# Branch sums in six PSUM banks and another order of the second block's rope factors, splits and taps

## What is computed

```python
# first block
h = rms_norm(x, mix_norm_g)
proj = h @ w_in                          # 1024 x 8708: four attentions' q, k, v and a gate of 4 x 1024
ys = mixers(proj)                        # stick-breaking, dilated, forgetting, differential: 4 x 256 wide
branch = einsum('bsnc,ncd->bsnd', ys, w_branch)
x = x + sum_n(sigmoid(gate_n) * branch_n) @ w_out
x = x + square(relu(rms_norm(x, mlp_norm_g) @ w_up)) @ w_down
x = rms_norm(x, final_norm_g)
# second block
h = rms_norm(x, norm1_g)
q, k, v, u = split(h @ w_in_2)           # 512, 512, 512, 2 x 512
q, k = rope(rms_norm(q)), rope(rms_norm(k))      # per head of 64
attn = causal_softmax_attention(q, k, v)         # 8 heads, one block of 256 keys
a, g = split(u + glu_b);  h = a * sigmoid(g)
conv = silu(layer_norm(causal_depthwise_conv31(h) + dw_b))
x = x + concat(attn, conv) @ w_out_2
x = x + (silu(h2 @ w_gate_2) * (h2 @ w_up_2)) @ w_down_2   # h2 = rms_norm(x, norm2_g)
```

## Time and profile before

| | |
|---|---|
| median of 3 runs | 815.37 us |
| the profiled execution | 815.08 us, its span 813.3 us |
| TensorE busy | 785.4 us, 97% of the span |
| VectorE busy | 476.2 us, 59% |
| ScalarE busy | 407.0 us, 50% |
| GpSimd busy | 41.8 us, 5% |
| read from memory | 134.43 MB, 167 GB/s over the span |
| mean granted TensorE clock | 0.998 of 2.4 GHz |

### The profile page before, as it was taken

How to read it: one execution, slowest core, us unless ns; L and a number is a source line. 1 busy time by engine, 2 the same in 40 slices (tenths; PEclk the granted TensorE clock), 3 DMA queues, 4 the chain that set the end, 5 groups by cost and what they waited for, 6 DMA issues and landing times.

```text
span 813.3 us, 9724 instructions
## 1 busy us (share of the span) xinstructions
PE 785.4 (97%) x3930; PEld 659.4 (81%) x3930; DVE 476.2 (59%) x623; ACT 407.0 (50%) x542; POOL 41.8 (5%) x38
## 2 busy tenths in 40 slices
PE   7999999999999899999999998998999999999998
PEld 5887889888888687888888887776987888888896
DVE  6654364757765867554445447688956645445534
ACT  6565455455656536455444445555455543443341
POOL 1000000000000410000000004011000000000000
PEclk9999999999999999999999999999999999999999
DMA  9842424434445355655655554835113755655341
GB/s 336 310 156 92 141 78 156 155 116 144 156 157 205 114 184 192 222 185 174 207 182 180 187 176 148 318 127 190 54 52 104 259 173 190 204 160 205 103 156 53
DMA packets 68508, 136.25 MB, mean 168 GB/s; under 512 B 2416, under 2 KB 7152, under 8 KB 67824
## 3 DMA queue, kind: packets, MB, share of 16 engines
q1 hardware_dynamic: 68000, 134.44, 48.3%
q10 hardware_dynamic: 464, 1.20, 0.4%
HBM read 134.43 MB, written 1.05 MB: 167 GB/s over the span
## 4 chain that ended last, share of the span: by engine, by line
PE 82%; DVE 9%; ACT 4%; issue 2%; POOL 1%; DMA 0%; ACTq 0%; SPq 0%; DVEq 0%
PE b L574 19%; PE b L576 18%; PE b L575 18%; PE SS L574 4%; PE SS L576 4%; PE SS L575 4%; PE TT L543 4%; DVE ca L1956 2%; DVE wlo L1492 2%; PE OO L576 2%; PE OO L574 2%; PE OO L575 2%; ACT whi L1054 1%; PE SS L657 1%; PE b L714 1%
## 5 line engine op out<-in xcount | busy, mean ns | idle before, releaser
L1492 DVE TENSOR_TENSOR wlo<-raw,whi 128x2048 fp32r<-128x2048 f32 (+2 forms) x123 | 273.8, 2228 | 160.2 <-ACT whi L1054 160.0
L1054 ACT CAST whi<-raw 128x2048 fp32r<-128x2048 f32 (+2 forms) x123 | 227.3, 1850 | 125.8 <-PE b L576 86.9
L574 PE MATMUL b<-whi,Ahi 128*128 128x512 f32 (+2 forms) x568 | 222.8, 392 | 3.1 <-DVE wlo L1492 1.8
L576 PE MATMUL b<-whi,Alo 128*128 128x512 f32 (+2 forms) x568 | 216.2, 381 | 0.0
L575 PE MATMUL b<-wlo,Ahi 128*128 128x512 f32 (+2 forms) x568 | 215.7, 380 | 0.0
L574 PEld LDWEIGHTS b<-whi,Ahi 128*128 128x128 f32 x568 | 107.9, 190 | 23.4 <-issue 2.5
L576 PEld LDWEIGHTS b<-whi,Alo 128*128 128x128 f32 x568 | 107.5, 189 | 20.8
L575 PEld LDWEIGHTS b<-wlo,Ahi 128*128 128x128 f32 x568 | 108.0, 190 | 18.5
L574 PE MATMUL b<-whi,Bhi 128*128 128x512 f32 x168 | 66.9, 398 | 3.0 <-DVE gates L1758 2.7
L576 PE MATMUL b<-whi,Blo 128*128 128x512 f32 x168 | 65.5, 390 | 0.0
L575 PE MATMUL b<-wlo,Bhi 128*128 128x512 f32 x168 | 65.5, 390 | 0.0
(11 more groups left out here) (270 smaller groups left out, 1000.0 us busy)
## 6 DMA issues: line engine op xcount, KB each, us to landing
raw<-in_w_in SPq DMA_DIRECT2D x40, 1024.0 KB, 4.9
raw<-in_w_up SPq DMA_DIRECT2D x16, 1024.0 KB, 5.4
raw<-in_w_dn SPq DMA_DIRECT2D x16, 1024.0 KB, 4.9
raw<-in_w_d SPq DMA_DIRECT2D x11, 1024.0 KB, 5.0
raw<-in_w_g SPq DMA_DIRECT2D x10, 1024.0 KB, 5.0
raw<-in_w_u SPq DMA_DIRECT2D x10, 1024.0 KB, 4.9
raw<-in_w_out SPq DMA_DIRECT2D x8, 1024.0 KB, 4.9
raw<-in_w_br SPq DMA_DIRECT2D x4, 1024.0 KB, 5.0
```

What stands on the lines that cost most here:

```text
L574: e.matmul(dst, xh, H[:, kc, c0:ce], start=first and kc == krs[0], stop=False)
L576: ins = e.matmul(dst, xl, H[:, kc, c0:ce], start=False, stop=last and kc == krs[-1])
L1054: e.copy(whi[:, s, 0:m], raw[:, r, 0:m]).then_inc(s_hi, 1)
L1492: e.tensor_tensor(wlo[:, s, 0:m], raw[:, r, 0:m], whi[:, s, 0:m].bitcast(F32), ALU.subtract).then_inc(s_lo, 1)
```

## The change

- **Banks.** The 16 groups of the branch stage go over six banks, 7, 0, 1, 2, 3, 4, instead of three; the two explicit entries of `gone` for banks 1 and 2 are dropped, since those banks' last branch groups are now recorded by the loop.
- **Timetable of the second block.** The turn of the gate half and its sigmoid (`gt`, `gs`) stand two groups later, the turn of the value half (`ut`) one group later, the gating `ug` at the same groups as before; the first two turns of rotated q (`r2`) one group earlier. Taps before the attention are 7 + 2 + 4 + 2 instead of 4 + 2 + 1 + 1.
- **Order on VectorE.** A rope factor stands before the group's split, `ug` behind everything else. In the norm steps the split stands between the gain product and the low part. At chunk 0 a split stands between the two parts of the statistics.
- **Order on ScalarE.** At chunk 0 the cast of the unit stands before the last turn's steps and the four final squares. The table of exponentials is loaded behind group 7.
- **Attention.** Six taps a head instead of seven; the rounds 8 and 9 of TensorE are written out, with the seventh head's product before the eighth head's turn.

```diff
--- before.py
+++ after.py
@@ -64,9 +64,12 @@
          9: [(0, "v", 1280, None)]}
 
 QP = [(c, col, dst, sc) for c in range(10) for col, kind, dst, sc in PAIRS[c] if kind == "qk"]
+
 CH2 = [(2048, 512), (1536, 512), (0, 512), (512, 512), (1024, 512)]
 HC2 = [4, 4, 4, 4, 4, 2]
 W_ACC = {(0, 0): 3, (1, 0): 4, (0, 1): 7, (1, 1): 0}
+
+BR = [7, 0, 1, 2, 3, 4]
 FIRST = [(0, 0), (1, 0), (0, 1), (1, 1)]
 PLAIN = [(0, 0), (0, 1), (1, 0), (1, 1)]
 
@@ -129,19 +132,21 @@
 def timetable2():
 
 
-    bg = {s: [] for s in range(24)}
-    bg[3] += [("gt", 0)]
-    bg[4] += [("gs", 0), ("gt", 1)]
-    bg[5] += [("gs", 1)]
-    bg[7] += [("ut", 0)]
-    bg[8] += [("ut", 1), ("ug", 0)]
-    bg[9] += [("ug", 1)]
-    for i, (a, b, c) in enumerate(((11, 13, 15), (12, 14, 16), (15, 17, 18), (16, 18, 19))):
+    bg = {s: [] for s in range(20)}
+    bg[5] += [("gt", 0)]
+    bg[6] += [("gs", 0), ("gt", 1)]
+    bg[7] += [("gs", 1)]
+    bg[8] += [("ut", 0), ("ug", 0)]
+    bg[9] += [("ut", 1), ("ug", 1)]
+    for i, (a, b, c) in enumerate(((11, 13, 14), (12, 14, 15), (15, 17, 18), (16, 18, 19))):
         bg[a] += [("r0", i), ("ra", i)]
         bg[b].append(("r1", i))
         bg[c].append(("r2", i))
-    for s, n in ((10, 4), (11, 2), (13, 1), (14, 1)):
+    for s, n in ((10, 7), (12, 2), (14, 4), (18, 2)):
         bg[s].append(("cv", n))
+    rank = {"r1": 0, "ug": 0, "r0": 1, "ra": 1}
+    for s in bg:
+        bg[s].sort(key=lambda x: rank.get(x[0], 2))
     return bg
 
 
@@ -781,7 +786,7 @@
             for n in range(4):
                 for t in range(2):
                     g = 8 * hf + 2 * n + t
-                    bk = g % 3
+                    bk = BR[g % 6]
                     w.wait_ge(s_xl, X["B", t, n // 2] + 1)
                     clear(bk)
                     product(("br", hf, n, t), Bhi, Blo, 4 * (n // 2), t, lambda c0, bk=bk: bank[bk], True, True,
@@ -841,8 +846,6 @@
                     tail(k)
 
 
-        gone[1] = (s_gm, 14)
-        gone[2] = (s_gm, 15)
         for j in range(8):
             def turn_h(j=j):
                 for t in range(2):
@@ -948,16 +951,20 @@
             conv(n_conv[0])
             n_conv[0] += 1
 
-        for k in range(10):
-            if k < 8:
-                az(k)
-                tile_part()
-            if 1 <= k < 9:
+        for k in range(8):
+            az(k)
+            tile_part()
+            if k:
                 at(k - 1)
-            if k < 4 or k > 7:
+            if k < 4:
                 tile_part()
             if k > 1:
                 ap(k - 2)
+        tile_part()
+        ap(6)
+        at(7)
+        tile_part()
+        ap(7)
         tile_part()
         for t in range(2):
             key = ("Y", t, 0)
@@ -1397,16 +1404,19 @@
 
         for i in range(5):
             for q, (ui, t) in enumerate(PLAIN):
-                if i == 0 and q == 0:
-                    turn2(1, 1)
-                    for t_, n_ in ORD:
-                        fin_square(t_, n_)
                 if q == 0 and i:
                     evac2(i - 1, 1)
                 if q == 3:
                     evac2(i, 0)
                 after("p2", i, ui, t)
+                if i == 0 and q == 0:
+                    turn2(1, 1)
+                    for t_, n_ in ORD:
+                        fin_square(t_, n_)
                 stages2(4 * i + q)
+                if 4 * i + q == 7:
+
+                    e.preload_act_table_set("natural_log_exp_and_others")
         evac2(4, 1)
         for k in range(10):
             if k < 8:
@@ -1748,7 +1758,7 @@
             g = 8 * hf + 2 * n + t
             sg = gates[:, t, 1024 * n + 512 * hf:1024 * n + 512 * hf + 512]
             mx = ys[:, t, 512 * hf:512 * hf + 512]
-            bk = bank[g % 3]
+            bk = bank[BR[g % 6]]
             w.wait_ge(s_mm, done("br", hf, n, t))
             w.wait_ge(s_sig, 4 * hf + n + 1)
             if n == 0:
@@ -1776,11 +1786,14 @@
             xs = xr[:, t, 512 * n:512 * n + 512]
             e.tensor_tensor(xs, xs, bank[W_ACC[t, n]], ALU.add).then_inc(s_res, 1)
 
-        def gained(key, col):
+        def gained(key, col, between=None):
+
             dst = tg[:, XG[key] % 2, :].rearrange("p (k q) -> p k q", k=4)
             if XG[key] >= 6:
                 w.wait_ge(s_xl, X[[q for q in XG if XG[q] == XG[key] - 2][0]] + 1)
             x_gain(key, col, dst)
+            if between:
+                between()
             x_lo(key, dst)
 
         def out_proj(name, norm, base, gain):
@@ -1803,8 +1816,9 @@
                 residual(base, t, n)
                 if k:
                     p = ORD[k - 1]
-                    gained((norm, *p), pcol(gain, 4 * p[1], 4))
-                before(name, 1, n, t)
+                    gained((norm, *p), pcol(gain, 4 * p[1], 4), lambda: before(name, 1, n, t))
+                else:
+                    before(name, 1, n, t)
 
         out_proj("wo", "N1", 0, "g_mlp")
 
@@ -1853,20 +1867,22 @@
             if 0 < j < 7:
                 hidden_lo(j)
 
-        def turn2(t, n):
-            gained(("N2", t, n), gg[:, 4 * n:4 * n + 4])
+        def turn2(t, n, between=None):
+            gained(("N2", t, n), gg[:, 4 * n:4 * n + 4], between)
 
         w.wait_ge(s_sq, SQ["N1", 1, 1] + 1)
         for k, (t, n) in enumerate(ORD):
             w.wait_ge(s_mm, done("dn", 7, n, t))
             residual(4, t, n)
             if k:
-                turn2(*ORD[k - 1])
-            before("dn", 7, n, t)
+                turn2(*ORD[k - 1], lambda: before("dn", 7, n, t))
+            else:
+                before("dn", 7, n, t)
 
 
         def stats2():
             stats("r3", o3, SQ["N2", 1, 1] + 1)
+            before("p2", 0, 0, 1)
             sm_, v, r = smx["r4"]
             o4v = o4.rearrange("p (t n) -> p t n", n=2)
             w.wait_ge(s_sq, SQ["F", 1, 1] + 1)
@@ -1978,27 +1994,30 @@
                     r0(i)
                 elif name == "ra":
                     ra(i)
-                elif name == "r1":
-                    r1(i)
-                elif name == "ug":
-                    ug(i)
                 elif name == "cv":
                     conv(i)
 
         for i in range(5):
             for q, (ui, t) in enumerate(PLAIN):
-                before("p2", i, ui, t)
+                for name, h in BG2[4 * i + q]:
+                    if name == "r1":
+                        r1(h)
                 if i == 0 and q == 0:
+                    before("p2", 0, ui, t)
                     turn2(1, 1)
                     k_x = stats2()
+                before("p2", i, ui, t)
                 stages2(4 * i + q)
+                for name, h in BG2[4 * i + q]:
+                    if name == "ug":
+                        ug(h)
         before("wo2", 0, 0, 0)
         for k in range(10):
             if k < 8:
                 am(k)
             if 1 <= k < 9:
                 at(k - 1)
-            conv(7 if k < 8 else 1)
+            conv(6 if k < 8 else 1)
         x_lo(("Y", 0, 0))
         x_lo(("Y", 1, 0))
         w.wait_ge(s_cp, NT)
```

## The result

| | before | changed |
|---|---|---|
| median of 8 runs each | 815.3 us (815.04 to 819.17) | 811.86 us (809.01 to 812.39) |
| ratio, 95% interval | | 0.9934, 0.9913 to 0.9956 |
| the profiled execution, its span | 815.08, 813.3 us | 809.01, 807.2 us |
| mean granted TensorE clock of the executions | 0.998 (profiled) | 1.0 once, 0.998 twice, 0.993 or 0.994 five times |

The change makes the kernel 0.66% faster. I forecast 806.1 us and 804.0 to 810.0. The sign was right; the median lies 5.8 us above the forecast and 1.9 above the range. Two gaps of about equal size make it up: the profiled execution has gained 6.06 us, not 9.3, and it is the shortest of the eight; the usual one takes 2.9 us more at a lower mean clock.

The account below looks back on a forecast made before the run. TensorE was taken to bound the kernel, with 82% of the chain of waits, through its stalls and a slow clock stretch. Terms -2.8 - 0.4 - 4.2 - 1.9 = -9.3 from 815.08 gave a median of 806.1 us, range 804.0 to 810.0.

Parts of the forecast that it names:

- Branches: Branch stage: with six banks both stalls behind gate products go, -3.2 from start to start, net -2.8 us (bounds 0, -3.2).
- It takes back 0.35: w_out: the split for its second unit ends at 288.4, TensorE wants it at 288.1, so 0.35 us is lost again.
- Split between gain product and low part: Norm of the attention output: VectorE's splits fill waiting time, the ReLU TensorE waited for is done in time; -0.4 us (0, -0.5).
- Down product to the attention: Second block up to the attention: attention starts 4.2 us earlier, term -4.2 (bounds -3.5 and -5.1).
- last gain product to scale: VectorE at chunk 0: takes 6.7 us instead of 6.0, from 498.2 to 499.9, so the scale comes at 504.9 to 506.6.
- Chunk 3's stall: Ahead of chunk 3: value half's turn comes only 2.3 us earlier, its 12.65 us chain is unchanged; stall grows from 0.67 to 3.5.
- The rope chain: Chunk 3 to third turn of query and key: VectorE sets the pace; one split leaves, two taps enter, idle goes; 1.9 us shorter.
- Attention: Attention: six taps shorten VectorE's pace to 7 x 2.96 us, the 1.63 stall goes; term -1.9 (bounds 0, -2.0).
- On these rows I leave it at 2.4 GHz: TensorE's clock: no fall expected, since none followed the 3.25 us stall; a fall before chunk 3 would make 806.3 us.
- Rival 1: Chunk 1: scale as late as before, clock still falls; term +1.3 instead of -4.2, 811.6 us; 7%.
- Rival 4: Chunk 1: one clock fall at its remaining stall delays the gating chain by 1.7 us; 807.8 us; 8%.
- Rivals 2, 3, 5 and 6: 2: VectorE holds branches, 808.9, 6%; 3: attention gains nothing, 808.0, 8%; 5: scale in time, 805.2, 12%; 6: slower, 823, 2%.

Follow-up runs that it names:

- the trace of 813.19: Changed kernel measured again, unaltered: profiled execution 813.19 us at a clock of 0.992; median 812.07 us, ratio 0.9941.
- three edits more: Changed kernel with copies late, plus value half turned one group earlier, w_out's second split ahead of the mix, half a split between the statistics: 803.3 us, ratio 0.9823.
- the late copies alone: Changed kernel with ScalarE's four issues of shifted copies and two casts of constants moved from behind the second gating to behind group 13: 808.77 us, ratio 0.9902.

## Why the forecast was right in sign and too low

**Branches, -2.8 forecast, -2.0 measured.** Both stalls went and 3.4 us with them. The failed step is "It takes back 0.35": it took back 1.4. I had the split of w_out's second unit reach VectorE 1.1 us earlier than the earlier trace rows; it began at 286.82 instead of 287.33, 0.5 earlier. The split before it came earlier too, beside one of GpSimd's additions, and took 3.01 instead of 2.28, and the wait for GpSimd ahead of the mix grew from 0.30 to 0.95:

```profile
278.86 3.01 DVE L1502 TENSOR_TENSOR wlo<-raw,whi 128x2048 fp32r<-128x2048 f32 x1
...
285.21 1.69 DVE L1772 TENSOR_TENSOR ys<-ys,gates 128x512 f32<-128x512 f32 x1 [0.95 <-POOL ys L2117]
286.82 2.28 DVE L1502 TENSOR_TENSOR wlo<-raw,whi 128x2048 fp32r<-128x2048 f32 x1
```

The banks-only kernel shows the same stall, and the kernel with that split ahead of the mix has none.

**Split between gain product and low part, -0.4 forecast, -0.9 measured**, past its bound of -0.5. The cause is as argued: the kernel with the old order has the 0.30 stall back and is 0.9 later. I had counted the stall alone. The same order gives 0.3 more behind the second block's attention, where I had forecast no change.

**Down product to the attention, -4.2 forecast, -1.6 measured.** The stall ahead of chunk 0 shrank to 0.47, but not by the step that I gave for it, the split ahead of the low part: with that order taken back it is 0.67. The failed step is "last gain product to scale": I summed 6.7 us from durations taken alone and let it start at 498.2 to 499.9. It started at 500.9 on that axis, since a low part beside GpSimd's product took 1.78 us, and took 7.2, since the root took 2.67 instead of 0.70. So the scale came at 508.1, not at 504.9 to 506.6. For the split of the down product I had written a bound for GpSimd's work beside it; for the split between the statistics I wrote none. The kernel without that split shows the root at 0.70 and the stall as long, now behind the split. Cut in half, it gains 0.6 us.

**Chunk 3's stall.** Forecast 3.5 us, measured 3.38. Right, and so was its cause, as the kernel with the value half turned back shows: 0.66. The rope chain was forecast 1.9 shorter: from chunk 3's first product to the attention it took 26.1 instead of 28.1 us, 2.0 shorter. No run takes the order of the rope factors back alone.

**Attention, -1.9 forecast, -1.2 measured.** The stall of 1.63 went and two of 0.29 and 0.19 came behind ScalarE's evacuations (`ys`, L1389). Seven taps put back lengthen it by 1.6.

**The clock.** "On these rows I leave it at 2.4 GHz" failed. The profiled execution bears it out; none of the other seven does. A mean clock of 0.998 is one fall of 3.4 us, which two have, and 0.993 or 0.994 is about three, which five have. I took one fall that came and one that did not come, behind the 3.25 us stall, for a rule, from one execution. The Trainium skill's rule that I set against it ("TensorE: Matmul & The Clock Gate", section "HAM oscillation": a long idle gap throttles the array and the work behind it starts cold) was right in kind: six of nine traces with the 3.4 us stall ahead of chunk 3 have the fall. It is not certain either, three have none. The 3.25 us stall that I held against it has no fall behind it in either of its two traces, but it is shorter, and it says nothing of the 3.4 us stall; and falls come behind stalls of 2.1 to 2.4 us too, in eight of twelve. My price of it, nearly nothing, holds for a fall of 3.4 us and not for one of 6.8.

**The rivals.** Rival 1, scale as late as before and the clock still falling, 811.6 us, had 7%. Both its conditions hold in most executions, and the median is 811.86. That the times agree so well is in part luck. It wanted chunk 3 some 3.2 us later than before on the old axis; in the trace of 813.19, with its fall at chunk 1, it comes 2.0 later, and a fall of 1.3 at chunk 3, which the rival does not have, makes up the rest. Rival 4's fall came, with 1.6 us for my 1.7, and on top of rival 1's scale. Rivals 2, 3, 5 and 6 fell.

**What stays open.** Why the same program falls in one execution and not in the next; what the first 15 us vary by; whether w_out's stall changes the odds of a fall at chunk 1 (two pairs of traces don't tell); and what share of the executions without a profile had which fall, since they show a mean clock only.

## What to carry to other kernels

An instruction put into another engine's waiting time is only free if the two don't hinder each other: give every VectorE instruction with two SBUF inputs a bound for the GpSimd work beside it, and the other way round, and try it in halves. Take an engine's clock from several executions; one profile with no fall says little where stalls of over 2 us remain. And a side job in a queue, such as four DMA issues, belongs behind the evacuation that TensorE waits for: moving that, with three edits more, brought the ratio to the kernel before, each measured beside it on its own chip, from 0.9934 to 0.9823.

## What I had not expected

A GpSimd operation on 128x2 elements takes 0.70 us alone, 1.60 beside half a split and 2.67 beside a whole one. Between two executions of one program, clock falls alone make 4.5 us, 0.5%. What TensorE wins or loses can be evened out by an engine that is busier in the next stage: 1.4 of 3.7 us won with the late copies alone, 1.5 of 1.6 lost at a short clock fall.
